# Expert blocks whose token rows travel through DRAM buffers instead of one-hot matmuls, and small loads behind the second weight piece

## The chip, the core and the metric

The kernel runs on one core of one Trainium2 chip. The time is device microseconds (us) of one launch; the number that counts is the median of three runs. Beside the runs there is one execution recorded by the hardware profiler; it has its own time, and all rows below come from it.

The engines are named as in the profile: PE is TensorE (matmuls; PEld its weight loads), DVE is VectorE, ACT is ScalarE, POOL is GpSimd, SP is SyncE, which only issues transfers here. A q behind a name (SPq, POOLq) is that engine's instruction queue.

## The reference

Two decoder layers over 256 tokens of width 1024, all in float32, and a last RMSNorm. Each layer has an attention part (eight stick-breaking heads, four differential heads) and a feed-forward part; the first layer's is a dense SwiGLU of width 2816, the second's a mixture of eight SwiGLU experts of width 3584, of which each token uses two:

```python
logits = xf @ router_w                          # 256 x 8
top_logit, top_idx = lax.top_k(logits, 2)
gates = softmax(top_logit)
# tokens sorted by expert into blocks of 128 rows, each block of one expert
buf = zeros((cap, D)).at[dest].set(xf[sorted_tok])
yb = [swiglu(xb, w_gate[e], w_up[e], w_down[e]) for xb, e in blocks]
y = yb.reshape(cap, D)[dest] * sorted_gate[:, None]
out = segment_sum(y, sorted_tok)                # each token gets its two rows back
```

How many blocks there are depends on the data. With these inputs there are eight: the trace has 112 loads of gate pieces, 14 for each block.

## The kernel before

**Weights.** All weights are read once per use, in pieces of 1 MB (128 partitions x 2048 float32), 401 of them. SP loads them one after the other into a ring of seven buffers (`raw`); piece n is issued when the buffer of piece n-7 has been given back (`load`, line 343). A float32 matmul is done as three fast ones: ACT copies a piece rounded into `w_hi` (`split_hi`, line 327), DVE writes the rest `raw - w_hi` into `w_lo` (`split_lo`, line 332), both into rings of three buffers, and PE runs `mm3` (lines 437 to 439) over hi·hi, lo·hi and hi·lo. The activations are split in the same way (`aT_hi/aT_lo`, `xe_hi/xe_lo`, `he_hi/he_lo`, `ye_hi/ye_lo`).

**Order.** Every engine's program is written out by hand, and the engines meet in semaphores. In the program `piece_used` counts pieces that PE has finished, `lo_ready` those that DVE has split. Piece n can be split when PE has finished piece n-3.

**Start.** SP loads the two tiles of x and then pieces; ACT's queue loads the first gain and all constants (430 KB, with the identity that PE's transposes need); POOL issues ten small loads (bias tables, lambda vectors, head gains).

**Router.** After the last attention of layer 1 DVE normalises the rows (`hn`), PE transposes them (line 477) and forms the logits (line 666), and DVE picks the two experts by some 20 small operations (lines 1246 to 1271). Beside this POOL, ACT and DVE split `hn` into three bfloat16 parts `rows3` (lines 427, 429, 790, 1234), whose sum is exact.

**Expert block.** A block takes 42 pieces in chunks c = 0 to 7: chunk c has the gate and up pieces of 512 hidden columns and the down pieces of the chunk before. Its 128 input rows are gathered by matmuls: `gather` (line 689) multiplies `rows3` with a one-hot matrix `onehot`, 48 bfloat16 matmuls, in chunk 6 of the block before. Its output `ps[4:6]` is split into `ye_hi/ye_lo` and returned by `scatter` (line 698): eight matmuls with the transposed one-hot matrix, four after the second gate piece of the next block (t = 0) and four after its second up piece (t = 1), which need two transposes of `hot32` in chunk 2 (line 748), and two DVE additions into `xs` (`add_back`, line 1330). Block 0 is written out, blocks 1 to 6 are a loop on each engine, block 7 (the last) is written out.

In block 0 DVE works out the gates (chunk 1), the list of blocks (chunk 2) and the columns of each block (chunk 3), between its splits.

Of the kernel before, what the change touches and what calls it, by code (L numbers as in the profile page):

```python
# [19 lines left out]
F32 = mybir.dt.float32  # L20
# [7 lines left out]
P = 128  # L28
# [10 lines left out]
NE = 8  # L39
# [18 lines left out]
MAX_BLOCKS = S * 2 // P + NE - 1  # L58
TAB = MAX_BLOCKS + 1
# [51 lines left out]
def build(nc, x, w_in, w_out, attn_norm, ffn_norm, sb_out_norm, diff_subln, lambda_q1, lambda_k1,  # L111
          lambda_q2, lambda_k2, rel_bias, dense_w_gate, dense_w_up, dense_w_down, router_w,
          expert_w_gate, expert_w_up, expert_w_down, final_norm, consts, out):
    with ExitStack() as ctx:
# [61 lines left out]
        with ExitStack() as phase:  # L176
            hT_hi = sb("hT_hi", [P, FT, S], F32R, phase)
            hT_lo = sb("hT_lo", [P, FT, S], F32R, phase)

        until_experts.close()  # L180
        with ExitStack() as phase:
# [4 lines left out]
            rows3 = se("rows3", [P, 3, TT, D], BF16)  # L186
            onehot = se("onehot", [P, TT, P], BF16)
# [4 lines left out]
            ye_hi = se("ye_hi", [P, D], F32R)  # L192
# [3 lines left out]
            rT = se("rT", [P, KT, S])  # L196
# [28 lines left out]
            gate = se("gate", [P, TT, TAB])  # L225
            ebi = se("ebi", [P, TAB], I32)
            nbi = se("nbi", [P, 1], I32)

        scratch = nc.dram_tensor("bias_scratch", (DF_HEADS, 384), F32, kind="Internal").ap()
        ident = cst[:, C_ID:C_ID + P]  # L230
# [8 lines left out]
        cst_in, small_in, lam_ld, bkt_in = (sem(n) for n in ("cst_in", "small_in", "lam_ld", "bkt_in"))  # L239
        rw_in = sem("rw_in")  # L240
# [22 lines left out]
        part_done, rest_done = sem("part_done"), sem("rest_done")  # L263
# [4 lines left out]
        sc_done, sc_added = [sem("sc_done0"), sem("sc_done1")], [sem("sc_added0"), sem("sc_added1")]  # L268
        hot_t, hot_saved, hot_ready = (sem(n) for n in ("hot_t", "hot_saved", "hot_ready"))
# [69 lines left out]
        def _(sp):  # L339
# [8 lines left out]

            for n, src in enumerate(sources):
# [10 lines left out]
            load_block(0, slice(0, 1))  # L360
            sp.wait_ge(tab_done, 1)
            final = sp.value_load(nbi[0:1, 0:1], min_val=3, max_val=MAX_BLOCKS - 1)
            with sp.Fori(1, final + 1) as b:
                load_block(b, bass.ds(sp.value_load(ebi[0:1, bass.ds(b, 1)], min_val=0, max_val=NE - 1), 1))
            for t in range(TT):
                sp.wait_ge(out_rows, t + 1)
                sp.dma_start(out[0, t * P:t * P + P, :], hn[:, t, :]).then_inc(out_sent, 16)
# [4 lines left out]
        def _(pool):  # L372
            norms = [attn_norm[0], ffn_norm[0], attn_norm[1], ffn_norm[1], final_norm]

            def load_gain(m):
# [3 lines left out]
            pool.dma_start(bkt[:, 0:384], consts[0:N_BUCKETS + 1, C_OH:C_OH + 384]).then_inc(bkt_in, 16)  # L379
            pool.dma_start(bkt[0:N_BUCKETS, 384:384 + DF_HEADS], rel_bias[:, :]).then_inc(bkt_in, 16)  # L380
            pool.dma_start(bkt[N_BUCKETS:N_BUCKETS + 1, 384:384 + DF_HEADS],
                           consts[N_BUCKETS:N_BUCKETS + 1, C_MASKED:C_FLIP]).then_inc(bkt_in, 16)
            pool.dma_start(flip[:], consts[:, C_FLIP:C_END]).then_inc(bkt_in, 16)
            for i, v in enumerate((lambda_q1, lambda_q2, lambda_k1, lambda_k2)):
                pool.dma_start(lam_in[:, i], v.rearrange("l d -> (l d)").partition_broadcast(P)).then_inc(lam_ld, 16)
            pool.dma_start(g_sb[:].rearrange("p l d -> p (l d)"),
                           sb_out_norm.rearrange("l d -> (l d)").partition_broadcast(P)).then_inc(small_in, 16)
            pool.dma_start(g_df[:].rearrange("p l d -> p (l d)"),
                           diff_subln.rearrange("l d -> (l d)").partition_broadcast(P)).then_inc(small_in, 16)
# [14 lines left out]
            for l in range(DEPTH):  # L404
# [14 lines left out]
                if l == 0:  # L419
                    load_gain(2)  # L420
                    load_gain(3)
# [3 lines left out]
            for t in range(TT):  # L425
                pool.wait_ge(rows_done[t], 6)
# [987 lines left out]
```

## Time and profile before

| | us |
|---|---|
| median of the runs | 1552.97 (1551.99 to 1553.61) |
| the profiled execution | 1551.61 |
| its span, first to last instruction | 1549.9 |
| PE busy | 1450.6 (94%) |
| DVE busy | 1163.4 (75%) |
| ACT busy | 937.6 (60%) |
| moved by DMA | 427.52 MB, mean 276 GB/s |

The 1.7 us between span and time lie around the program. The busy shares are means over stages with different limits; the last two thirds of the span, from about 530 us on, are the eight expert blocks. PE's busy time is modelled at the ends of matmuls, so distances between starts say more than durations: a 512-column matmul is given with 0.39 us, and one starts every 0.227 us (883.63, 883.86, 884.09 us and so on). The stretches shown below are, in this order, one block of the loop, 34 us inside it, the start, and the first gather.

### The profile page before, as it was taken

The page shows a single profiled execution, that of the slowest core. Times are in us where ns is not written, and L with a number is a line of the kernel's source. Part 1 is how long each engine was busy: PE and PEld are TensorE (multiplying, and loading weights), DVE is VectorE, ACT ScalarE, POOL GpSimd, SP SyncE. Part 2 cuts the span into 40 slices and gives each one's busy share as a digit, 9 for nine tenths or more (in the row PEclk, how much of TensorE's full clock was granted, in tenths as well). Part 3 has the DMA queues.
Part 4 walks back from the last instruction along what each step waited for, and adds up shares of the span by engine and source line. Part 5 has one row for each costly group of instructions (what it writes and reads, how often), then busy time and mean ns, then how long its engine had stood idle before and what let it go on. Part 6 is the DMA issues. An engine that isn't in the chain of part 4 may idle for free.

```text
span 1549.9 us, 19815 instructions
## 1 busy us (share of the span) xinstructions
PE 1450.6 (94%) x7681; PEld 1226.9 (79%) x7681; DVE 1163.4 (75%) x884; ACT 937.6 (60%) x745; POOL 34.3 (2%) x60
## 2 busy tenths in 40 slices
PE   5997899998989699999999999999999999999996
PEld 4885899988867577778878878878878887887885
DVE  4547555545556799889888888979988988888886
ACT  4344343434444477667677767767766767776774
POOL 1110000000010100000000000000000000000000
PEclk9997999999998899999999999999999999999999
DMA  9641455555421399899989989989999999998991
GB/s 322 207 137 55 150 171 184 189 190 170 157 95 57 128 350 362 316 352 366 358 310 383 365 308 373 373 302 356 378 324 354 368 352 320 375 367 304 375 372 62
DMA packets 183299, 427.52 MB, mean 276 GB/s; under 512 B 6833, under 2 KB 8885, under 8 KB 183248
## 3 DMA queue, kind: packets, MB, share of 16 engines
q1 hardware_dynamic: 181840, 422.60, 76.2%
q0 software_dynamic: 1120, 3.24, 0.7%
q10 hardware_dynamic: 288, 0.96, 0.2%
q8 instruction: 37, 0.61, 0.2%
q14 instruction: 14, 0.11, 0.0%
HBM read 425.72 MB, written 1.05 MB: 275 GB/s over the span
## 4 chain that ended last, share of the span: by engine, by line
PE 87%; DVE 8%; ACT 2%; issue 1%; DMA 1%; ACTq 0%; DVEq 0%; SPq 0%
PE ps L437 27%; PE ps L439 26%; PE ps L438 26%; DVE w_lo L332 3%; PE ps L689 2%; PE ps L718 2%; ACT w_hi L327 1%; DMA raw<-in_w_in 1%; PE ps L698 1%; PE ps L511 1%; PE ps L477 1%; DVE hn L1033 1%; DVE aT_lo L1041 0%; DVE mx L1116 0%; DVE zb L1114 0%
## 5 line engine op out<-in xcount | busy, mean ns | idle before, releaser
L332 DVE TENSOR_TENSOR w_lo<-raw,w_hi 128x2048 fp32r<-128x2048 f32 x401 | 916.0, 2293 | 259.9 <-ACT w_hi L327 259.3
L327 ACT ACTIVATE w_hi<-raw 128x2048 fp32r<-128x2048 f32 x401 | 766.9, 1916 | 374.3 <-PE ps L439 368.3
L437 PE MATMUL ps<-w_hi,xe_hi 128*128 128x512 f32 x896 | 354.2, 395 | 6.8 <-DVE w_lo L332 6.8
L439 PE MATMUL ps<-w_hi,xe_lo 128*128 128x512 f32 x896 | 349.4, 390 | 0.0
L438 PE MATMUL ps<-w_lo,xe_hi 128*128 128x512 f32 x896 | 348.9, 389 | 0.0
L437 PEld LDWEIGHTS ps<-w_hi,xe_hi 128*128 128x128 f32 x896 | 168.3, 188 | 42.9 <-DVE w_lo L332 9.8
L439 PEld LDWEIGHTS ps<-w_hi,xe_lo 128*128 128x128 f32 x896 | 168.2, 188 | 35.7
L438 PEld LDWEIGHTS ps<-w_lo,xe_hi 128*128 128x128 f32 x896 | 168.4, 188 | 33.5
L437 PE MATMUL ps<-w_hi,he_hi 128*128 128x512 f32 x448 | 176.3, 394 | 17.4 <-DVE he_lo L1364 12.0
L437 PE MATMUL ps<-aT_hi,w_hi 128*128 128x256 f32 x608 | 175.0, 288 | 9.3 <-DVE aT_lo L1041 9.3
L439 PE MATMUL ps<-w_hi,he_lo 128*128 128x512 f32 x448 | 174.6, 390 | 0.0
L438 PE MATMUL ps<-w_lo,he_hi 128*128 128x512 f32 x448 | 174.4, 389 | 0.0
L438 PE MATMUL ps<-aT_lo,w_hi 128*128 128x256 f32 x608 | 173.9, 286 | 0.0
L439 PE MATMUL ps<-aT_hi,w_lo 128*128 128x256 f32 x608 | 173.8, 286 | 0.0
L437 PEld LDWEIGHTS ps<-aT_hi,w_hi 128*128 128x128 f32 x608 | 118.7, 195 | 11.5 <-DVE aT_lo L1041 10.4
L438 PEld LDWEIGHTS ps<-aT_lo,w_hi 128*128 128x128 f32 x608 | 118.8, 195 | 0.0
L439 PEld LDWEIGHTS ps<-aT_hi,w_lo 128*128 128x128 f32 x608 | 118.7, 195 | 0.0
L437 PEld LDWEIGHTS ps<-w_hi,he_hi 128*128 128x128 f32 x448 | 84.1, 188 | 40.6 <-issue 13.7
L439 PEld LDWEIGHTS ps<-w_hi,he_lo 128*128 128x128 f32 x448 | 84.1, 188 | 17.8
L438 PEld LDWEIGHTS ps<-w_lo,he_hi 128*128 128x128 f32 x448 | 84.1, 188 | 17.0
L790 ACT ACTIVATE he_hi<-ps 128x512 fp32r<-128x512 f32 x56 | 33.5, 599 | 80.1 <-PE ps L718 80.1
L437 PE MATMUL ps<-w_hi,aT_hi 128*128 128x512 f32 x128 | 50.9, 398 | 3.6 <-DVE aT_lo L1041 3.6
(207 smaller groups left out, 1124.1 us busy)
## 6 DMA issues: line engine op xcount, KB each, us to landing
raw<-in_expert_w_gate SPq DMA_DIRECT2D x112, 1024.0 KB, 6.3
raw<-in_expert_w_up SPq DMA_DIRECT2D x112, 1024.0 KB, 6.6
raw<-in_expert_w_down SPq DMA_DIRECT2D x112, 1024.0 KB, 6.5
raw<-in_w_in SPq DMA_DIRECT2D x24, 1024.0 KB, 6.8
raw<-in_dense_w_gate SPq DMA_DIRECT2D x11, 1024.0 KB, 5.1
raw<-in_dense_w_up SPq DMA_DIRECT2D x11, 1024.0 KB, 5.0
raw<-in_dense_w_down SPq DMA_DIRECT2D x11, 1024.0 KB, 4.9
raw<-in_w_out SPq DMA_DIRECT2D x8, 1024.0 KB, 5.0
```

The lines of the kernel that those rows point to most:

```text
L327: nc.scalar.activation(w_hi[:, n % SPL, :], raw[:, n % RAW, :], ACT.Copy).then_inc(hi_ready, 1)
L332: nc.vector.tensor_tensor(w_lo[:, n % SPL, :], raw[:, n % RAW, :], w_hi[:, n % SPL, :].bitcast(F32), ALU.subtract).then_inc(lo_ready, 1)
L437: pe.matmul(o, s_hi, m_hi, start=start, stop=False, skip_group_check=True)
L438: pe.matmul(o, s_hi, m_lo, start=False, stop=False, skip_group_check=True)
L439: return pe.matmul(o, s_lo, m_hi, start=False, stop=stop, skip_group_check=True)
L477: last = pe.transpose(ps[:, 4 + j, (2 * q + t) * P:(2 * q + t) * P + P], hn[:, t, (2 * j + q) * P:(2 * j + q) * P + P], ident)
L511: pe.matmul(bank[:, 0:ZW], neg_tri, spl[:, g % 2, m, :], start=False, stop=False, skip_group_check=True)
L689: last = pe.matmul(ps[:, 1 + 2 * j, q * P:q * P + P], rows3[:, part, t, k * P:k * P + P], onehot[:, t, :], start=(t == 0 and part == 0), s ...
L698: last = pe.matmul(ps[:, bank + c, :], onehotT[:, t, :], part[:, c * CH:c * CH + CH], start=(part is ye_hi), stop=(part is ye_lo), skip_gr ...
L718: last = pe.transpose(ps[:, 7, f * P:f * P + P], hid[:, c % 2, f * P:f * P + P], ident)
L790: return nc.scalar.activation(dst, src, ACT.Copy, scale=scale)
L1033: V.scalar_tensor_tensor(out=hn[:, t, :], in0=xs[:, t, :], scalar=row_fine[:, t:t + 1], in1=gain[:], op0=ALU.mult, op1=ALU.mult).then_inc( ...
```

## The change

1. `x_rows` and `y_rows` are DRAM buffers of 11 blocks of 128 rows of 4 KB. POOL clears an SBUF tile `zero` in layer 0, and SP fills both buffers with it, two stores of 512 KB behind each of the weight pieces 24 to 34.
2. In block 0 DVE computes for every token the row of its two places (`destinations`, chunk 3) and which of them lie before the last block (`rows_before_last`, chunk 4); the columns of the blocks move from chunk 3 to chunk 5. POOL then sends the rows of `hn` to `x_rows` by four indirect transfers.
3. For blocks 1 to 7 SP loads the block's rows (`xrow`, 512 KB) ahead of piece 32 of the block before, and PE turns them by eight transposes in chunk 6. The 48 matmuls of `gather` go. Block 0 alone is still gathered, by 16 float32 matmuls from `hn` and `hot32`.
4. ACT copies a block's output to `yrow`, and SP stores it to `y_rows` (512 KB) ahead of piece 12 of the next block. The scatter matmuls, `ye_lo`, `hot32`'s transposes, the one-hot tiles and both additions stay for the last block alone. In the last block POOL fetches the tokens' rows of the other blocks by four indirect transfers of 512 KB, and DVE adds them, two in chunk 4 and two in chunk 5.
5. `rows3` and the work on it by POOL, ACT and DVE go.
6. At the start the identity (64 KB) is loaded alone and first on ACT's queue; the other constants (366 KB) stand behind piece 0 on SP's queue, and the ten small loads go from POOL's queue to SP's, behind piece 1.

```diff
+            def small_loads():
+
+                sp.dma_start(bkt[:, 0:384], consts[0:N_BUCKETS + 1, C_OH:C_OH + 384]).then_inc(bkt_in, 16)
...
             for n, src in enumerate(sources):
                 load(n, src)
-
-            def load_block(b, e):
+                if n == 0:
+                    sp.dma_start(cst[:, P:CONSTS], consts[:, P:CONSTS]).then_inc(cst_in, 16)
+                if n == 1:
+                    small_loads()
+                if ZERO_AT <= n < ZERO_AT + MAX_BLOCKS:
+                    sp.wait_ge(zero_set, 1)
+                    sp.dma_start(x_blocks[n - ZERO_AT], zero[:]).then_inc(zeroed, 16)
+                    sp.dma_start(y_blocks[n - ZERO_AT], zero[:]).then_inc(zeroed, 16)
...
+                    if i == Y_STORE and not first:
+
+                        sp.wait_ge(y_saved, b)
+                        sp.dma_start(y_blocks[bass.ds(before, 1)].rearrange("b p d -> (b p) d"), yrow[:]).then_inc(y_sent, 16)
+                    if i == X_LOAD and not last_block:
+
+                        if first:
+                            sp.wait_ge(x_sent, 16 * 2 * TT)
+                        else:
+                            sp.wait_ge(y_sent, b * 16)
+                        sp.wait_ge(ga_done, b * 2 + 2)
+                        sp.dma_start(xrow[:], x_blocks[bass.ds(after, 1)].rearrange("b p d -> (b p) d")).then_inc(xrow_in, 16)
...
-            for t in range(TT):
-                pool.wait_ge(rows_done[t], 6)
-                nc.gpsimd.tensor_copy(rows3[:, 0, t], hn[:, t]).then_inc(part_done, 1)
-            pool.wait_ge(part_done, TT + 1)
-            nc.gpsimd.tensor_tensor(rows3[:, 2], hn[:], rows3[:, 1], ALU.subtract).then_inc(rest_done, 1)
             load_gain(4)
+            pool.wait_ge(zeroed, 32 * MAX_BLOCKS)
+            pool.wait_ge(dest_done, 1)
+            for i in range(2):
+                for t in range(TT):
+                    pool.indirect_dma_start(x_rows, bass.IndirectOffsetOnAxis(ap=dest_i[:, i, t:t + 1], axis=0),
+                                            hn[:, t, :], None).then_inc(x_sent, 16)
...
-            def gather(count):
-
-                pe.wait_ge(hot_ready, count)
+            def turn_gathered(b):
+
+                pe.wait_ge(xrow_in, b * 16 + 16)
+                for j in range(2):
+                    for q in range(4):
+                        k = 4 * j + q
+                        last = pe.transpose(ps[:, 1 + 2 * j, q * P:q * P + P], xrow[:, k * P:k * P + P], ident)
+                    last.then_inc(ga_done, 1)
...
-                    if c == 0 and not first:
-                        pe.wait_ge(y_lo, b)
-                        pe.wait_ge(hot_saved, b)
-                        scatter(0)
-                    if c == 1 and not first:
-                        pe.wait_ge(sc_added[1], b)
...
-                        gather(b + 2)
+                        turn_gathered(b)
...
+            def output_rows(b):
+
+                act.wait_ge(piece_used, nth(MOE0, b))
+                copy(yrow[:], both(ps[:, 4:6, :])).then_inc(y_saved, 1)
...
+            def add_rows(i, t):
+
+                dve.wait_ge(y_got[i][t], 16)
+                link(V.scalar_tensor_tensor(out=xs[:, t, :], in0=y_of[:, i, t, :], scalar=g_in[:, i, t:t + 1],
+                                            in1=xs[:, t, :], op0=ALU.mult, op1=ALU.add))
```

**PE in the loop over blocks, chunk 6**, behind the transposes of the hidden rows (`hid`); `xe_hi`, `xe_lo` are the block's input. First the kernel before:

```order
L718 MATMUL ps<-cst,hid 128x128 x4
L683 REGISTER_ALU
L689 MATMUL ps<-onehot,rows3 128x128 x48
L442 REGISTER_ALU
L437 MATMUL ps<-w_hi,xe_hi 128x512
```

and then the changed one:

```order
L787 MATMUL ps<-cst,hid 128x128 x4
L745 ISA
L749 MATMUL ps<-cst,xrow 128x128 x8
L502 REGISTER_ALU
L497 MATMUL ps<-w_hi,xe_hi 128x512
```

The 48 gather matmuls are replaced by eight transposes of the loaded rows, at the same place.

**DVE at the head of a block in the loop**, chunk 0 and the start of chunk 1; `ye_lo` belongs to the output of the block before, `xs` holds the tokens' sums. First the kernel before:

```order
L332 TENSOR_TENSOR w_lo<-raw,w_hi 128x2048
L1325 TENSOR_TENSOR ye_lo<-ps,ye_hi 128x1024
L331 REGISTER_ALU
L332 TENSOR_TENSOR w_lo<-raw,w_hi 128x2048
L1330 ISA
L1330 SCALAR_TENSOR_TENSOR xs<-ps,gate,xs 128x1024
L331 REGISTER_ALU
L332 TENSOR_TENSOR w_lo<-raw,w_hi 128x2048
```

and then the changed one:

```order
L349 TENSOR_TENSOR w_lo<-raw,w_hi 128x2048
L348 REGISTER_ALU
L349 TENSOR_TENSOR w_lo<-raw,w_hi 128x2048
L348 REGISTER_ALU
L349 TENSOR_TENSOR w_lo<-raw,w_hi 128x2048
```

Nothing stands between the splits any more; the addition for t = 1, which came in chunk 1 before, is gone as well.

**SP at the start**, from the tiles of x to the third weight piece. Before the change the two tiles are followed by the pieces alone. First the kernel before:

```order
L341 DMA xs<-in_x 128x1024 x2
L347 DMA raw<-in_w_in 128x4x512 x12
```

and then the changed one, in full up to piece 2:

```order
L358 DMA xs<-in_x 128x1024 x2
L364 DMA raw<-in_w_in 128x4x512
L383 DMA cst<-in_consts 128x732
L364 DMA raw<-in_w_in 128x4x512
L368 DMA bkt<-in_consts 33x384
L369 DMA bkt<-in_rel_bias 32x4
L370 DMA bkt<-in_consts 1x4
L372 DMA flip<-in_consts 128x128
L374 DMA lam_in<-in_lambda_q1 128x128
L374 DMA lam_in<-in_lambda_q2 128x128
L374 DMA lam_in<-in_lambda_k1 128x128
L374 DMA lam_in<-in_lambda_k2 128x128
L375 DMA g_sb<-in_sb_out_norm 128x128
L377 DMA g_df<-in_diff_subln 128x256
L364 DMA raw<-in_w_in 128x4x512 x10
```

The ten small loads stand ahead of pieces 2 to 11, and the constants ahead of piece 1.

## Rows read from the trace of the kernel before

**Rows 1.** Stretches: us, busy by engine (PE, PEld, DVE, ACT, POOL), PEclk, DMA share, GB/s

```profile
781.00:907.00 126.00, 123.23 (x592) 101.68 (x591) 109.64 (x67) 89.08 (x60) 0.00 (x0) 1.00 0.97 350
816.00:850.00 34.00, 34.00 (x156) 28.21 (x155) 30.24 (x18) 24.97 (x16) 0.00 (x0) 1.00 1.03 385
0.00:17.00 17.00, 3.91 (x16) 3.14 (x16) 3.89 (x11) 4.77 (x10) 5.67 (x14) 1.00 0.87 236
525.00:529.60 4.60, 4.60 (x46) 4.60 (x45) 2.96 (x3) 0.60 (x1) 0.00 (x0) 0.50 0.27 61
```

**Rows 2.** Chain of waits, 880 to 1020 us (start us, us, what)

```profile
886.95 2.68 PE ps L689 x48
...
916.60 2.29 DVE w_lo L332
918.93 0.50 PE ps L437
...
1012.95 2.68 PE ps L689 x48
```

**Rows 3.** PE's timeline (start us, us, ..., in brackets idle before and releaser)

```profile
563.92 0.60 PE L718 MATMUL ps<-cst,hid 128*128 128x128 f32 x4
564.35 0.38 PE L748 MATMUL ps<-cst,hot 128*128 128x128 f32 x2
...
902.55 0.47 PE L437 MATMUL ps<-w_hi,he_hi 128*128 128x512 f32 x1 [1.50 <-DVE he_lo L1364]
...
914.17 0.39 PE L698 MATMUL ps<-ye_hi,onehotT 128*128 128x512 f32 x1
```

**Rows 4.** DVE's timeline, head of a block

```profile
915.39 1.28 DVE L1330 SCALAR_TENSOR_TENSOR xs<-ps,gate,xs 128x1024 f32<-128x1024 f32 x1 [1.31 <-PE ps L698]
```

**Rows 5.** DVE's timeline in the router

```profile
506.82 1.02 DVE L1020 SCALAR_TENSOR_TENSOR row_tmp<-row_rstd 128x1 f32<-128x1 f32 x1
...
517.19 3.92 DVE L1251 TENSOR_TENSOR rk<-eq,cst 128x16 f32<-128x16 f32 x1
...
522.18 0.17 DVE L1251 TENSOR_TENSOR rk<-eq,cst 128x16 f32<-128x16 f32 x1
```

**Rows 6.** POOL's timeline in the router

```profile
517.01 4.07 POOL L429 TENSOR_TENSOR rows<-hn,rows 128x2048 bf16<-128x2048 f32 x1 [6.36 <-ACT rows L790]
521.02 0.56 POOL L377 DMA_DIRECT2D gain<-in_final_norm  x1
```

**Rows 7.** PE's timeline: small float32 matmuls, and the first gather

```profile
476.50 1.06 PE L593 MATMUL ps<-v_df,wT 128*128 128x128 f32 x4
...
524.82 5.23 PE L689 MATMUL ps<-onehot,rows 128*128 128x128 bf16 x48 [1.49 <-DVE onehot L1268]
529.86 0.48 PE L437 MATMUL ps<-w_hi,xe_hi 128*128 128x512 f32 x1
```

**Rows 8.** Timeline of the start

```profile
16.80 1.91 ACT L327 ACTIVATE w_hi<-raw 128x2048 fp32r<-128x2048 f32 x1 [6.04 <-DMA raw<-in_w_in]
...
22.29 0.58 PE L437 MATMUL ps<-aT_hi,w_hi 128*128 128x256 f32 x1 [7.53 <-DVE aT_lo L1041]
```

**Rows 9.** The page: GB/s that the transfers moved, in 40 equal slices of 38.7 us

```profile
GB/s 322 207 137 55 150 171 184 189 190 170 157 95 57 128 350 362 316 352 366 358 310 383 365 308 373 373 302 356 378 324 354 368 352 320 375 367 304 375 372 62
```

**Rows 10.** Block 0, chunk 3: DVE's extra work, and PE behind it

```profile
584.66 0.25 DVE L1311 TENSOR_TENSOR tmpb<-cm,posm 128x96 f32<-128x96 f32 x1
...
587.39 6.70 DVE L332 TENSOR_TENSOR w_lo<-raw,w_hi 128x2048 fp32r<-128x2048 f32 x3
...
589.74 0.50 PE L437 MATMUL ps<-w_hi,he_hi 128*128 128x512 f32 x1 [1.28 <-DVE w_lo L332]
```

**Rows 11.** A piece's way: SP's issue, ACT's use, landing times of one block's pieces

```profile
849.14 0.37 SPq L347 DMA_DIRECT2D raw<-in_expert_w_up  x1
...
864.30 1.92 ACT L327 ACTIVATE w_hi<-raw 128x2048 fp32r<-128x2048 f32 x1 [0.80 <-PE ps L439]
...
DMA to landing us min/median/max: 5.1/7.3/9.1
```

More of the change, by code:

```diff
@@ L58 @@
 MAX_BLOCKS = S * 2 // P + NE - 1
+ZERO_AT = 24
+Y_STORE, X_LOAD = 12, 32
 TAB = MAX_BLOCKS + 1
@@ L185, in build @@
             xe_lo = se("xe_lo", [P, KT, P], F32R)
-            rows3 = se("rows3", [P, 3, TT, D], BF16)
-            onehot = se("onehot", [P, TT, P], BF16)
+            y_of = se("y_of", [P, 2, TT, D])
+            ye_hi = se("ye_hi", [P, D], F32R)
+            with ExitStack() as router:
+                rT = sb("rT", [P, KT, S], F32, router)
+            xrow = se("xrow", [P, D])
+            yrow = se("yrow", [P, D])
             hot32 = se("hot32", [P, TT, P])
@@ L420, in _ @@
                     load_gain(2)
+                    nc.gpsimd.memset(zero[:], 0.0).then_inc(zero_set, 1)
                     load_gain(3)
@@ L687, in gather @@
                         for t in range(TT):
-                            for part in range(3):
-                                last = pe.matmul(ps[:, 1 + 2 * j, q * P:q * P + P], rows3[:, part, t, k * P:k * P + P],
-                                                 onehot[:, t, :], start=(t == 0 and part == 0), stop=(t == 1 and part == 2),
-                                                 skip_group_check=True)
+                            last = pe.matmul(ps[:, 1 + 2 * j, q * P:q * P + P], hn[:, t, k * P:k * P + P],
+                                             hot32[:, t, :], start=(t == 0), stop=(t == TT - 1), skip_group_check=True)
                     last.then_inc(ga_done, 1)
@@ L754, in expert_block @@
                         expert_in("up", c, 1)
-                    if c == 0 and not first:
-                        pe.wait_ge(sc_added[0], b)
-                        scatter(1)
+                    if c == 1 and not first:
+                        pe.wait_ge(y_saved, b)
                     if c > 0:
@@ L1354, in expert_block @@
                         lo_of("up", c, 0)
-                        if c == 0 and not first:
-                            add_back(b, 0).then_inc(sc_added[0], 1)
                         lo_of("up", c, 1)
@@ L1373, in expert_block @@
                     if first and c == 3:
+                        destinations()
+                    if first and c == 4:
+                        rows_before_last()
+                    if first and c == 5:
                         block_columns()
-                    if c == 4 and not last_block:
-                        one_hot(lambda t: sel[:, t, bass.ds(b + 1, 1)])
+                    if last_block and c in (4, 5):
+                        for t in range(TT):
+                            add_rows(c - 4, t)
                     if 0 < c < E_CH:
```

133 lines of the change are left out of this document (84 added, 49 removed).

## The prediction

> **What bounds the kernel now.** I began with the stretches. One block of the loop lasts 126 us with PE busy for 123.2, DVE for 109.6, ACT for 89.1, and the DMA engines at a share of 0.97 with 350 GB/s [rows 1]. So PE sets the pace, DVE has some 13% to spare, and the transfers have little: that is the first thing to see here. Then the chain of waits: it lies on PE in the blocks, and the gathers of two neighbouring blocks start at 886.95 and 1012.95, 126.00 us apart [rows 2]. Whatever leaves PE's program in a block therefore shortens the kernel seven times, as long as the splits (ACT, then DVE) and the transfers keep up. Last, PE's timeline shows where it stands idle in a block: 1.50 us at the end, for `he_lo` [rows 3], and about 1.1 us at the head, for a split [rows 2].
>
> **Head of a block (7 times).** At 914.17 PE starts the four matmuls of the first scatter [rows 3], and only at 918.93 the second up piece [rows 2]. Between them lies one piece, 12 matmuls at 0.227 = 2.72 us. So 4.76 - 2.72 = 2.04 us go: 0.91 for the scatter and 1.13 of waiting for the split that DVE starts at 916.60 [rows 2], behind the addition at 915.39 [rows 4]. The second scatter is another 4 x 0.227 = 0.91 us. Does the wait come back in another form? DVE had been idle for 1.31 us before 915.39, so the split of the first up piece was done at 914.1; PE now comes for it at 914.17. The next split would end at 914.1 + 2.3 = 916.4, and PE needs it at 914.17 + 2.72 = 916.9. It just fits. ACT's copy of the output stays (into `yrow` instead of `ye_hi`, the same size). Gain 2.95 us, x7 = 20.7. The end with the wait left in place is 1.82 x 7 = 12.7.
>
> **Chunk 6 (7 times).** 48 matmuls take 2.68 us [rows 2]. Eight transposes of 128x128 float32 take 0.108 us each, since four of them on `hid` run from 563.92 to 564.35 [rows 3]: 0.86 us. Gain 1.82, x7 = 12.7. The two transposes of the one-hot tile in chunk 2, of the same kind [rows 3], go too: 0.22 x 7 = 1.5. At half speed the eight would take 1.7 us, which would leave 6.8 of the 12.7.
>
> The 1.50 us at a block's end stay: transposes, `he_hi`, `he_lo` are not touched.
>
> **Router (once).** POOL's subtraction runs from 517.01 to 521.08 [rows 6], and DVE's `rk`, 128x16, lasts 3.92 us beside it where its twin lasts 0.17 [rows 5]. `row_tmp`, of one column, lasts 1.02 us [rows 5] beside POOL's first cast; I give it the same 0.17 without. Both stand on the way from the norm to the logits and the choice. With POOL's work gone I take off 3.75 + 0.85 = 4.6 us. POOL's issue of a transfer does not do this: 521.02 to 521.58 [rows 6] DVE's small steps keep their length. Against it stands the first gather. Before, 48 bfloat16 matmuls from 524.82 to 529.86 [rows 7], at the 1.2 GHz level (PEclk 0.50, [rows 1]); at the 2.4 GHz level they take 2.68 [rows 2]. PE had had little to do before. The new one has 16 float32 matmuls of 128x128, each of two records (line 593 is such a product, and its two matmuls are x4 in [rows 7]). A record of this size takes 0.108 at the high level [rows 3] and so 0.216 at the low one: 32 of them 6.9 us, 1.8 more than before, or 3.5, 1.6 less. PE idles for some 4 us less now, so either is possible; I take the low level. Net -2.8 (the other end -6.2).
>
> **Start (once).** PE's first weight matmul starts at 22.29, 5.5 us behind ACT's first split, which had waited for piece 0 until 16.80 [rows 8]. Ahead of or beside this piece everything flowed: x, a gain, the constants, ten small loads. Now 1 MB of x, 512 KB of gain, the identity's 64 KB and the piece stand there, 2.69 MB. At the 322 GB/s of the first slice [rows 9], and with data from about 2 us on, the piece lands at 10.4; I take 10.5, so 6.3 earlier. Ends: at the 385 GB/s of the blocks 9.0 (-7.8); at the 236 that the first 17 us had, small packets among them [rows 1], 13.4 (-3.4). x's second tile comes earlier by its share, and the row norms finish just ahead of the split. The small loads stand behind pieces 0 and 1 and land by about 18 us; PE first asks for the bias tables behind the two pieces of its first product, DVE for the lambda vectors behind three splits: in time. Piece 2 follows at about 20 us and is needed when PE has done two pieces, 96 matmuls, behind 16 us: in time too.
>
> **What is added.** The 22 stores of zeros, 11.5 MB behind 11 pieces, double the load of a stage that moves 184 to 190 GB/s [rows 9]. 380 at most is just below the 385 of [rows 1], and seven buffers at 5.5 us a piece are far ahead there: nothing (to 2). Clearing `zero` on POOL may hold DVE up once, as the cast did: 0.2 (0 to 1). In block 0 the extra steps of chunk 3 took 587.39 - 584.66 = 2.73 us and made PE wait 1.28 [rows 10], so 1.45 us in a chunk cost nothing. `destinations` has 7 steps of 0.2 (0.17 and the hand-over), `rows_before_last` 4: both fit, and the block columns cost in chunk 5 what they cost in chunk 3: 0 (to 1.5). In the last block DVE adds two rows of 1.28 us [rows 4] in each of two chunks: 2.56 - 1.45 = 1.1, x2 = +2.2 (0 to 5).
>
> The waits that are new stand on SP and POOL. Behind SP's wait for `x_sent` all weight pieces from 32 on are queued. POOL can send from about 586 us, SP arrives some 16 us later, six pieces on; four transfers of 512 KB at an issue of 0.56 each [rows 6] and 9.1 us to land [rows 11] need 11 to 12, or 17 if they share the engines evenly with the weights. If they are late by a few us, the ring covers it: a piece issued at 849.14 is taken by ACT at 864.30, 15.2 us later, and takes 7.3 to land, 9.1 at worst [rows 11]. In the last block POOL's fetch has over 25 us before DVE asks for it.
>
> **Sum.** -20.7 - 12.7 - 1.5 - 2.8 - 6.3 + 0.2 + 0 + 2.2 = -41.6. The profiled execution, 1551.61 us, would be 1510.0; the median of the runs is 1.36 above it, and I predict 1552.97 - 41.6 = **1511.4**.
>
> **Rivals.** *The transfers become the bound.* A block now moves 42 pieces and two half pieces, 45.1 MB, and is to last 126.0 - 5.0 = 121.0 us: 373 GB/s. For it speaks the row of the block: 350 GB/s at a share of 0.97 is 361 at full share, which gives 124.9 us a block, only 1.1 gained. Against it: 385 GB/s for 34 us on end, at a share of 1.03, so the share is no ceiling [rows 1]; and the slack of 6 to 8 us of [rows 11]. At 385 the block needs 117 us of transfers. With 361 the three block terms shrink from 34.9 to 7.7 and the time is 1538. The Trainium skill says in DMA: Bandwidth & Descriptors, section "Where 436 GB/s comes from", that HBM gives a core about 358 GB/s and that this binds; by it a block would take 126.0 us and nothing would be gained in the blocks, 1546. By that rule the 385 of this trace could not be; its section on measured bandwidth allows more with the other core idle, as here, and the trace agrees with that.
>
> *A split takes the place of the wait at the head.* The fit is 0.1 and 0.5 us. If DVE is late there as before, 1.13 x 7 = 7.9 comes back: 1519.
>
> *Slower than before.* POOL issues the indirect transfers, each to 128 addresses that it must take one by one from a table. What that costs is shown by no row. If the four take T us from 586 on, SP holds all weights back and PE starves once T is over 16 + 8 = 24 us. It outweighs the 41.6 from T = 66 on, 16 us for each transfer, where the nearest row has 0.56 for an issue of 128 rows. At T = 80 the time would be 1511.4 + 56 = 1567.
>
> *The change does not do what it says*, say PE waits for `xrow` in each block: SP issues that load ten pieces ahead, 29 us, so I give it nothing of its own.
>
> **How the numbers follow.** Forecast 0.66 (its own range 1505 to 1520), split late 0.12 (1519), transfers bound 0.14 (1520 to 1546, mostly 1538), slower 0.04, faster than forecast (gather at the high level, start at 385 GB/s) 0.04, about 1505. The range 1504 to 1528 leaves out nearly all of the slow case, most of the transfer case and a little below. About 0.2% is what a measurement tells from no change. Faster 0.95, same 0.01, slower 0.04.
>
> **What would show it.** ACT's first split near 10.5 us and PE's first weight matmul near 16. `rk` at 0.17 us. Blocks of the loop 121 us apart, with no wait at the head and 1.50 us at the end. The wait of ACT's splits for `raw` in the blocks: none, if I am right; some in each block, growing to the last, if the transfers bind. Idle of about 1.1 us on PE twice in the last block. Wrong would be a distance of blocks of 125 or more, or SP waiting long at `x_sent`.

## The result and the profile after

The changed kernel takes 1511.17 us (median of 4 runs, 1510.65 to 1512.92) against 1553.29 (4 runs, 1551.99 to 1554.19): a ratio of 0.973, 95% interval 0.9715 to 0.9748. Predicted were 1511.4 with a range of 1504 to 1528. The profiled execution took 1511.28 with a span of 1509.5, against 1551.61 and 1549.9; the steps below are taken from these two.

The same place of PE's program, in both traces (us from the span's start; the lead is the difference):

| PE's start of | before | after | lead |
|---|---|---|---|
| first weight matmul | 22.29 | 15.91 | 6.38 |
| last weight matmul ahead of the router | 503.64 | 498.85 | 4.79 |
| transposes of the logits | 516.25 | 510.62 | 5.63 |
| first gather | 524.82 | 515.35 | 9.47 |
| first weight matmul of block 0 | 529.86 | 521.55 | 8.31 |
| last hidden tile of block 0 | 648.45 | 638.19 | 10.26 |
| first hidden tile of block 1 | 676.16 | 662.91 | 13.25 |
| first hidden tile of the last block | 1432.08 | 1388.64 | 43.44 |
| last hidden tile of the last block | 1527.66 | 1487.34 | 40.32 |

So nearly all of it comes from the blocks. From one block of the loop to the next it is 120.95 us, as against 126.00 in [rows 2] (121.0 was predicted). Stretches of the trace after: one block, 34 us inside one, and the start (engines' busy time and, last, PEclk, DMA share and GB/s), to be read against [rows 1]:

```profile
882.22:1003.19 120.97, 119.13 (x541) 98.10 (x541) 105.14 (x58) 89.05 (x60) 0.00 (x0) 1.00 1.01 373
789.00:823.00 34.00, 34.00 (x156) 28.14 (x155) 30.10 (x18) 25.16 (x17) 0.00 (x0) 1.00 1.04 395
0.00:17.00 17.00, 4.53 (x21) 4.02 (x22) 8.48 (x17) 10.29 (x15) 0.20 (x4) 0.96 0.81 268
```

PE is busy for 119.1 of 121.0 us, and the transfers run at the 373 GB/s that the new pace needs. The waits from 640 to 1390 us, which are the end of block 0 and the six blocks of the loop (what waited and for whom; total, times, longest):

```profile
ACT w_hi L344 <- PE ps L499: 115.9, 184, 1.2
...
PE ps L497 <- DVE he_lo L1436: 10.5, 7, 1.5
...
PE ps L497 <- DVE w_lo L349: 2.2, 7, 0.3
```

No split waits for `raw`. What is left on PE is the stop of 1.5 us at each block's end, which [rows 3] showed and which was not touched, and a short one behind it. The start, on the chain of waits (start, us, what), answers to [rows 8]:

```profile
1.72 8.63 DMA raw<-in_w_in
10.38 1.92 ACT w_hi L344
12.32 2.29 DVE w_lo L349
14.61 1.21 DVE aT_lo L1105 x2
15.91 0.55 PE ps L497
```

The router on DVE, to be read against [rows 5]; `row_tmp` and `rk` now last what their twins did:

```profile
502.02 0.16 DVE L1084 SCALAR_TENSOR_TENSOR row_tmp<-row_rstd 128x1 f32<-128x1 f32 x1
...
511.57 0.17 DVE L1312 TENSOR_TENSOR rk<-eq,cst 128x16 f32<-128x16 f32 x1
```

POOL's timeline at the indirect transfers, the operation that no row of before showed, and SP's wait for them:

```profile
578.41 2.20 POOL L476 DMA_INDIRECT x_rows<-hn,dest_i  x1 [73.67 <-DVE dest_i L1370]
580.92 1.86 POOL L476 DMA_INDIRECT x_rows<-hn,dest_i  x1 [0.30 <-issue]
583.08 1.99 POOL L476 DMA_INDIRECT x_rows<-hn,dest_i  x1 [0.30 <-issue]
585.38 2.58 POOL L476 DMA_INDIRECT x_rows<-hn,dest_i  x1 [0.30 <-issue]
```

```profile
SPq L407 <- DMA x_rows<-hn,dest_i: 3.4, 1, 3.4
```

An issue costs 1.9 to 2.6 us, three to five times the 0.56 of [rows 6]. From the first issue to the last landing, 596.1, it is 17.7 us. The ring hides it, but barely: the weight piece issued at 597.0, right behind SP's wait, landed at 610.4 and ACT took it at 611.0, 0.6 us later. In the loop this slack is 5.1 to 13.6 us. Most of it was gone before SP waited: the pieces issued at 581.9 to 589.9, while the rows were on their way, had 1.0 to 1.1 us left when they landed. From 588 to 597 us the transfers moved 412 GB/s.

Last, the end of the chain in the last block, where rows are added (start, us, what):

```profile
1440.92 0.68 DVE he_lo L1436
1441.60 1.20 DVE xs L1382
1442.83 1.30 DVE xs L1382
1444.24 2.30 DVE w_lo L349
1446.58 0.50 PE ps L497
```

The chunk with this stop lasts 18.32 us where its neighbours last 16.81, and the next one 18.37: 3.1 us in all, which is the step down from 43.44 to 40.32 in the table.

### The profile page after: what moved, and what is told of

Read it like the earlier page. It is cut to its first block, busy times and chain, and to the rows that moved or that the text cites. A ratio compares the mean times of both kernels' runs of the same rounds, so it can differ in the third digit from the quotient of the medians.

```text
span 1509.5 us, 19091 instructions
## 1 busy us (share of the span) xinstructions
PE 1421.4 (94%) x7315; PEld 1199.9 (79%) x7315; DVE 1130.3 (75%) x842; ACT 935.7 (62%) x744; POOL 42.6 (3%) x58
## 4 chain that ended last, share of the span: by engine, by line
PE 87%; DVE 8%; ACT 2%; issue 1%; DMA 1%; ACTq 0%; SPq 0%; DVEq 0%
PE ps L497 28%; PE ps L499 27%; PE ps L498 27%; DVE w_lo L349 3%; ACT w_hi L344 2%; PE ps L787 1%; PE ps L573 1%; DVE aT_lo L1105 1%; DMA raw<-in_w_in 1%; DVE hn L1097 1%; PE ps L537 0%; PE ps L759 0%; DVE mx L1180 0%; DVE zb L1178 0%; PE ps L749 0%
## 5 line engine op out<-in xcount | busy, mean ns | idle before, releaser
L497 PE MATMUL ps<-w_hi,he_hi 128*128 128x512 f32 x448 | 176.8, 395 | 19.8 <-DVE he_lo L1436 12.0
```

Of the source, the lines that this page charges most:

```text
L497: pe.matmul(o, s_hi, m_hi, start=start, stop=False, skip_group_check=True)
```

## The experiments

Each was run 5 times if nothing else is said, beside the kernel before on the same chip. The medians of that are 1553.56 for start_only, pool_router, head_add and spread, 1554.12 for extra2, extra4, early and early_spread, and 1552.95, on another chip, for start_cst, send_thrice, more_zeros and busy_router. The changed kernel was not run again in these groups; what is said against it is against its 1511.17 above. As the kernel before moved by 1.2 us from group to group, a difference of about 1 us between medians of different groups says nothing by itself.

| run | us | lowest to highest | ratio to before, 95% |
|---|---|---|---|
| start_only | 1548.07 | 1545.5 to 1548.61 | 0.9942 to 0.9970 |
| start_cst (11 runs) | 1552.26 | 1549.27 to 1554.71 | 0.9987 to 1.0005 |
| pool_router | 1515.86 | 1514.59 to 1516.97 | 0.9743 to 0.9770 |
| head_add | 1514.83 | 1514.58 to 1515.74 | 0.9738 to 0.9765 |
| spread | 1508.74 | 1507.65 to 1509.55 | 0.9695 to 0.9722 |
| extra2 | 1510.57 | 1507.88 to 1512.47 | 0.9709 to 0.9735 |
| extra4 (4 runs) | 1534.01 | 1532.44 to 1535.66 | 0.9858 to 0.9888 |
| send_thrice | 1521.76 | 1520.62 to 1523.22 | 0.9782 to 0.9808 |
| more_zeros | 1512.33 | 1510.87 to 1513.27 | 0.9721 to 0.9747 |
| early | 1491.85 | 1488.61 to 1494.37 | 0.9584 to 0.9613 |
| early_spread | 1489.14 | 1486.36 to 1490.76 | 0.9568 to 0.9594 |
| busy_router | 1487.44 | 1486.80 to 1487.53 | 0.9562 to 0.9588 |

**The start alone (start_only).** The kernel before, with

```
                 load(n, src)
+                if n == 0:
+                    sp.dma_start(cst[:, P:CONSTS], consts[:, P:CONSTS]).then_inc(cst_in, 16)
+                if n == 1:
+                    small_loads()
...
+            act.dma_start(cst[:, C_ID:C_ID + P], consts[:, C_ID:C_ID + P]).then_inc(ident_in, 16)
             act.dma_start(gain[:], attn_norm[0].partition_broadcast(P)).then_inc(gain_first, 16)
-            act.dma_start(cst[:], consts[:, 0:CONSTS]).then_inc(cst_in, 16)
```

and without the ten small loads on POOL's queue.

> The kernel before with the start of the changed one and nothing else. Theory: the first piece and the small loads stood in each other's way; PE's first weight matmul moves from 22.29 to about 15.9 (6.4 us). Of that the changed kernel still has 5.65 at its router, and I put the 0.7 that it loses on the way to the clock's windows, which fall otherwise over the attention; then this kernel loses them too and ends 5.6 us below the kernel before, near 1547.7. Rival: the 0.7 was taken by the zeros (clearing the tile, 22 stores), which are not here; then it ends 6.4 to 7 below, near 1546.5. Second rival: the start's gain needs the changed kernel's other tiles; then no first split near 10.4 here.

PE's first weight matmul came at 15.97 and the median is 5.5 us below before, near the 5.6 expected; on the way the trace lost more than the 0.7 that this rested on. The zeros are not in it, and yet of the 6.3 us of lead only 3.9 stood at the last weight matmul ahead of the router (499.71 against 503.64). So the rival with the zeros falls; the lead is lost elsewhere, see the clock below.

**Which part of the start (start_cst).** As above, without `small_loads()` in SP's queue: the ten small loads stay with POOL.

> The kernel before, with the identity loaded by itself and the other constants behind piece 0, but the ten small loads still on POOL's queue at the start. It tells apart what of the 6.3 us is due to the constants (366 KB moved back) and what to the small loads. Theory of the prediction (all bytes that flow beside the piece count alike, at 322 GB/s): 366 KB are 1.2 us, so ACT's first split comes at about 15.6 in place of 16.80, and the small loads, 0.58 MB, take the rest, most of it because they are small. Rival: the constants held the piece back by more than their bytes, and the split comes at 12 to 13.

ACT's timeline of this run:

```profile
16.14 1.91 ACT L328 ACTIVATE w_hi<-raw 128x2048 fp32r<-128x2048 f32 x1 [6.75 <-DMA raw<-in_w_in]
```

0.66 us earlier than 16.80 [rows 8]; start_only has this step at 10.44. So 5.7 of the 6.4 us come from where the small loads stood. At 322 GB/s their 0.58 MB would be 1.8 us: they cost three times that. Whether that is because they were issued beside the piece or because POOL's queue carried them is not told apart, since start_only changes both. In the medians start_cst can't be told from before. My expectation, which counted bytes, had the split at 15.6. The prediction itself did not hang on this: it took the 16.80 of before as it stood and gave the new start, in which no small load is left ahead of the piece, the rate of the first slice. The piece landed at 10.35 and 10.4 was worked out.

**POOL beside DVE (pool_router).** The changed kernel with POOL's old work in the router, into a tile that nobody reads:

```
+            for t in range(TT):
+                pool.wait_ge(rows_done[t], 6)
+                nc.gpsimd.tensor_copy(cast[:, 0, t], hn[:, t]).then_inc(cast_done, 1)
+            pool.wait_ge(lg_done, 1)
+            pool.wait_ge(cast_done, 2)
+            nc.gpsimd.tensor_tensor(cast[:, 1], hn[:], cast[:, 0], ALU.subtract).then_inc(cast_done, 1)
```

> The changed kernel, with POOL's two casts and its subtraction of 128x2048 put back in the router (into a tile that nobody reads). Theory: a step of DVE that meets POOL's subtraction is held until it ends; one DVE step of the choice lasts about 3.9 us again and one step of the norm about 1.0, so +4.6 us, near 1515.8. The clock may take or give about 1.5 of it at the first gather. Rival: rk was long for another reason (its place in the chain, the wait for the logits), and POOL costs nothing: 1511.2.

+4.7 us, as expected. DVE's and POOL's timelines of this run:

```profile
510.62 0.17 DVE L1319 TENSOR_REDUCE m<-lg 128x2 f32<-128x16 f32 x1
510.83 3.72 DVE L1320 TENSOR_TENSOR eq<-lg,m 128x16 f32<-128x16 f32 x1
514.58 0.17 DVE L1321 TENSOR_TENSOR rk<-eq,cst 128x16 f32<-128x16 f32 x1
```

```profile
510.46 4.05 POOL L478 TENSOR_TENSOR y_of<-hn,y_of 128x2048 bf16<-128x2048 f32 x1 [6.01 <-PE ps L741]
```

This time `eq` is held and `rk` is not, so it is no property of `rk`: the tensor-tensor step that meets POOL's subtraction ends with it (514.55 and 514.51; spans on POOL are rough). The reduction at 510.62 runs within POOL's instruction at its usual 0.17. The Trainium skill, SBUF — State Buffer, section "Terms", says that the port pair which DVE and GpSimd share is held for a whole instruction and that the loser fully blocks; the rows of `eq` and of POOL's subtraction agree.

**The wait at the head (head_add).** In the blocks of the loop, behind the split of the first up piece:

```
+                        if c == 0 and not first and not last_block:
+                            V.scalar_tensor_tensor(out=y_of[:, 0, 0, :], in0=xs[:, 0, :], scalar=gate[:, 0, 0:1],
+                                                   in1=xs[:, 1, :], op0=ALU.mult, op1=ALU.add)
```

> The changed kernel, with one step of DVE of 1.28 us (an addition of 128x1024 that nobody reads) behind the split of the first up piece in each of the six blocks of the loop, where the addition of the scatter stood, and no scatter. Theory: DVE has 0.1 us to spare at the first up piece and 0.5 at the second, so PE waits 1.28 - 0.5 = 0.8 for the second: 6 x 0.8 = +4.8 us, near 1516.0. Rival: the wait of 1.13 at the head came from the hand-over between PE's scatter and DVE, not from DVE's time; then nothing here, 1511.2. Second rival: DVE never makes the step up before the block ends; then 1.28 x 6 = 7.7, near 1518.9.

Blocks of the loop are 121.63 to 121.67 us apart against 120.95 to 120.97: 0.70 each, +3.7 us in the medians. PE's timeline of this run:

```profile
1019.34 0.50 PE L497 MATMUL ps<-w_hi,xe_hi 128*128 128x512 f32 x1 [0.38 <-DVE w_lo L349]
```

The expectation had 0.8 each. So the wait was DVE's time, and DVE has 0.6 us to spare there (0.5 was read). The rest of the old 1.13, 0.4 us, I put to DVE's having to wait for PE's scatter, 1.31 us in [rows 4]; no run shows that part by itself.

**Additions and columns spread (spread).**

```
-                    if first and c == 5:
-                        block_columns()
-                    if last_block and c in (4, 5):
-                        for t in range(TT):
-                            add_rows(c - 4, t)
+                    if first and c in (5, 6):
+                        block_columns(c - 5)
+                    if last_block and c in (3, 4, 5, 6):
+                        add_rows((c - 3) // TT, (c - 3) % TT)
```

> The changed kernel, with one row added in each of the chunks 3 to 6 of the last block instead of two in chunks 4 and 5, and the block columns of block 0 half in chunk 5 and half in chunk 6. Theory: a chunk hides 1.45 us of DVE's time, and one addition takes 1.28 and half of the columns 1.37; then the two stops of about 1.55 each in the last block and the one in block 0 all go: -4.6 us, near 1506.6. Rival: DVE has no such spare time in a chunk, its debt passes on to the next piece; then the four stops are of about 0.8 each and the time stays near 1511.

Measured: -2.4 us in the medians, and in the trace -3.6 behind the start of block 0. The chunks of the last block last 16.99 to 17.05 in place of 18.35, with 16.81 undisturbed, and chunk 5 of block 0 17.04 in place of 18.38. So a chunk hides about 1.1 us of DVE's time, not 1.45. That figure had been 2.73 - 1.28 from [rows 10]; but the chunk there was 1.58 longer than its neighbours. A row's bracket counts idle time from the modelled end of the matmul before, 0.39 behind its start, where the next one would have started after 0.23; and the pair of matmuls behind a stop is 0.34 apart, not 0.23. Both are left out of the 1.28. 2.73 - 1.58 is 1.15, and 2.64 - 1.15 is the 1.5 us of each stop in the last block.

**How much the transfers carry (extra2, extra4).** Two and four more loads of 1 MB in each of the blocks 0 to 6:

```
+                    if i in places and not last_block:
+                        j = places.index(i)
+                        ...
+                        sp.dma_start(y_of[:, j % 2], edown_v[0, :, 0:2, :]).then_inc(extra_in, 16)
```

> The changed kernel, with two more transfers of 1 MB in each of the blocks 0 to 6 (weights that nobody reads, into the buffer of the rows that come back, which lies idle there). A block then moves 47.2 MB in 120.95 us, 390 GB/s, against 373. Theory (transfers were never the bound, and can sustain about the 385 to 397 GB/s of the best slices): the ring of seven pieces loses its slack, PE waits at most 1 us a block: 1511 to 1518. Rival (361 GB/s is the ceiling, and the changed kernel lives on slack from before): 47.2 / 361 = 130.8 us a block, +69 us, near 1580.

> As before with four more transfers of 1 MB in each of the blocks 0 to 6: 49.3 MB, 408 GB/s if the block stayed at 120.95 us. Theory: this is above what any slice showed (397); at 397 a block takes 124.2 us, +3.2 x 7 = +23, near 1534. If the engines could carry well over 400, nothing happens: 1511. At 385 it is 128.1 us a block, +50, 1561. The time gives the ceiling itself.

The stretch from 640 to 1360 us, first of extra2, then of extra4:

```profile
640.00:1360.00 720.00, 710.86 (x3223) 585.91 (x3224) 626.73 (x345) 529.92 (x351) 0.00 (x0) 1.00 1.03 392
```

```profile
640.00:1360.00 720.00, 698.20 (x3126) 565.59 (x3127) 607.68 (x335) 518.23 (x342) 0.00 (x0) 1.00 1.04 396
```

With two more, blocks stay 120.95 us apart at 392 GB/s. With four they take 124.1 to 124.35, and the splits wait for `raw`, as this row of extra4's waits has it:

```profile
ACT w_hi L346 <- DMA raw<-in_expert_w_up: 58.5, 40, 3.4
```

49.3 MB in 124.1 to 124.35 us are 396 to 397 GB/s, and that is what these loads of 1 MB sustain. That 1534 came out to the microsecond is luck in part: the forecast had seven blocks of +3.2, while the trace has six of +3.2 to +3.4, 1.0 in the last block and 1.1 ahead of block 0. The changed kernel at 373 stands 6% below the limit. The rival at 361 is refuted. The Trainium skill, Perfetto Trace Analysis, section "Roofline", takes about 120% of 358 GB/s as the practical ceiling of a core alone. That is 430 GB/s, an estimate from its figures; here the limit in pieces of 1 MB was 397, 111%, though for 20 us of send_thrice, below, the transfers moved 415.

**The indirect transfers (send_thrice).**

```
-                            sp.wait_ge(x_sent, 16 * 2 * TT)
+                            sp.wait_ge(x_sent, 16 * 6 * TT)
...
-            for i in range(2):
-                for t in range(TT):
-                    pool.indirect_dma_start(x_rows, ...)
+            for rows in (x_rows2, x_rows3, x_rows):
+                for i in range(2):
+                    for t in range(TT):
+                        pool.indirect_dma_start(rows, ...)
```

> The changed kernel, with the four indirect transfers of token rows issued three times (twice into other DRAM buffers that nobody reads, then into x_rows); SP waits for all twelve. In the changed kernel an issue takes 1.9 to 2.6 us and the last of four lands about 10 us after it, SP waits 3.4 us, and the pieces behind it land 0.6 us before ACT takes them, against 7 in other chunks: the cover was nearly used up. Theory of the prediction (SP is held until the last transfer has landed, and the ring gives that time back only up to the piece's landing): twelve issues end at 608, the last lands at about 617, and the piece that SP then issues is wanted by ACT at 608.7 and takes 8 to land: PE stands 16 us, 1527. Rival (only the bytes count: 4.2 MB more at 397 GB/s): +10.6, 1522. Second rival: the ring has more to give than I read, under +5, 1515.

+10.6 us, where the theory said 16; block 0 to block 1 is 134.17 us in place of 124.89, +9.3. SP's wait (19.8 us in place of 3.4):

```profile
SPq L409 <- DMA x_rows<-hn,dest_i: 19.8, 1, 19.8
```

SP came free at 613.7 rather than 617, and its first piece landed at 619.6, 5.9 us later and not 8. Block 0 starts 1.8 us later in this execution, so ACT would have taken the piece at 610.5: 9.1 us late, close to the 9.3 measured. But SP's wait made little of that. ACT already stood for three pieces that SP had issued at 586.0, 588.9 and 591.6, ahead of its wait:

```profile
603.40 1.92 ACT L346 ACTIVATE w_hi<-raw 128x2048 fp32r<-128x2048 f32 x1 [2.33 <-DMA raw<-in_expert_w_gate]
609.82 1.92 ACT L346 ACTIVATE w_hi<-raw 128x2048 fp32r<-128x2048 f32 x1 [4.50 <-DMA raw<-in_expert_w_up]
614.53 1.91 ACT L346 ACTIVATE w_hi<-raw 128x2048 fp32r<-128x2048 f32 x1 [2.79 <-DMA raw<-in_expert_w_up]
```

By the same reckoning the third of them was 7.6 us late. Meanwhile the transfers ran without a pause, and only then did SP's wait leave them short of work (590 to 610 us, and 610 to 614):

```profile
590.00:610.00 20.00, 19.03 (x86) 15.42 (x85) 14.73 (x12) 10.74 (x8) 14.15 (x8) 1.00 1.04 415
610.00:614.00 4.00, 1.20 (x8) 0.78 (x6) 2.23 (x1) 1.74 (x1) 0.00 (x0) 1.00 0.60 241
```

So the rows' bytes, ahead of or among the weights', made about 7.6 of the 9.3 us, as the rival had it, and the theory's hold of SP at most the 1.7 left. An estimate from these rows fits: the 4.2 MB added are 10.1 us at 415 GB/s, less the 1.0 of slack. POOL's eight further issues do not set the time here, since the transfers were never idle behind them. Two stretches at the low clock, from 614.9 and from 625.1, each behind a stop of PE, are part of what was lost. Shown is that the slack of the changed kernel at this place was used up.

**More zeros (more_zeros).** A third store beside each round of two, into a buffer that nobody reads:

```
+                    sp.dma_start(spare_blocks[n - ZERO_AT], zero[:]).then_inc(zeroed, 16)
```

> The changed kernel, with 11 more stores of zeros (17.3 MB in 33 stores in place of 11.5 in 22, the third of each round into a buffer that nobody reads). Theory: 11 pieces and 33 stores are 28.8 MB, 73 us at 397 GB/s, on 60 us of PE's work; the ring is 12 us behind after it, and it had some 38 to spare in this stage, so nothing changes: 1511. Rival: the stage is near its limit already and the 22 stores cost the changed kernel something; then the 11 more cost up to 12 us.

1512.33: no difference that can be told. From the first weight matmuls of the stage at 170 us to the ones at 368 it is 198.4 us in both traces. The stores are free, with room.

**The stop that was left (early, early_spread).** In chunk 6 PE now runs

```
                     if c > 0:
                         expert_down(c - 1, 0)
+                        if c == E_CH - 1:
+                            turn_hidden(c)
                         expert_down(c - 1, 1)
```

with `he_hi` and `he_lo` of this one tile in the idle halves of `ye_lo`, and each half of `gathered` moved behind `he_lo` and behind the last split.

> The changed kernel, with the last hidden tile of a block transposed between the two pieces of the down product before it (in buffers of its own), so that he_hi and he_lo are made while PE works; ACT's and DVE's halves of the next gathered tile are moved behind it. Theory: the two stops that stayed at the end of a block, 1.55 us for he_lo and 0.47 for the next split, are hand-over and not DVE's load, so they go: 2.0 x 8 = -16 us, near 1495. A block then lasts 118.9 us and needs 379 GB/s, which the transfers carry. Rival: DVE has no time to spare there (six splits of 2.29, hid, he_lo and two gathered halves on 16.3 us of PE's work), and what goes at he_lo comes back at the next two or three splits: half of it, near 1503. If a block's transfers bind at 373 GB/s: nothing, 1511.

> The run before together with the spread additions and block columns. Theory: the two do not touch the same chunks but one (chunk 6), so the gains add: 2.4 for the spread as measured and up to 16: near 1493. Rival: the last addition and half of the columns now stand in the chunk in which the early transposes use up DVE's spare time, and about 1 us of it comes back.

1491.85, 19.3 us below the changed kernel; 1489.14 with the spreading. Blocks are 118.6 us apart: 2.35 us less each rather than 2.0. Some 0.15 of the rest lies in the pair of matmuls behind a stop, whose distance is 0.31 to 0.34 where it is 0.23 elsewhere; the last 0.2 I can't place. PE's timeline of early, where 1.50 us of idle time stood:

```profile
990.36 0.40 PE L505 MATMUL ps<-w_hi,he_lo 128*128 128x512 f32 x1
990.59 0.60 PE L793 MATMUL ps<-cst,hid 128*128 128x128 f32 x4
990.95 0.47 PE L503 MATMUL ps<-w_hi,he_hi 128*128 128x512 f32 x1
```

and 640 to 1360 us of early, in which PE has no idle time at all:

```profile
640.00:1360.00 720.00, 720.00 (x3278) 595.32 (x3277) 636.88 (x353) 541.29 (x359) 0.00 (x0) 1.00 1.03 381
```

**The clock in the router (busy_router).** early_spread with products that nobody reads in PE's pauses, such as

```
+                if l == DEPTH - 1:
+                    for _ in range(12):
+                        pe.matmul(ps[:, 7, :], aT_hi[:, 0, 0:P], aT_hi[:, 0:2, :].rearrange("p a s -> p (a s)"),
+                                  start=True, stop=True, skip_group_check=True)
                 turn_rows(3 * l + 2)
```

> The kernel of the run early_spread, with 24 products that nobody reads where PE waits in the router: 12 ahead of the last transposes, 8 behind the transposes of the logits, 4 ahead of the first gather. In early_spread the granted clock falls to 0.5 from 504.0 to 507.4 and from 514.2 to 521.1, and the first gather takes 6.2 us there. Theory: PE did little before each fall, and with these products the clock stays at 1.0; the gather takes 3.5 and the logits' product about 1 less: -3.7 us, near 1485.5. Rival: the added products stand ahead of the real ones and delay them by more than the clock gives, or the clock falls all the same: 1489 to 1491.

From the last weight matmul ahead of the router to the first of block 0, first busy_router, then early_spread:

```profile
499.84:519.48 19.64, 18.11 (x109) 13.81 (x108) 13.53 (x36) 8.36 (x16) 1.50 (x2) 1.00 0.42 137
```

```profile
499.09:521.76 22.67, 14.39 (x73) 10.51 (x72) 13.53 (x36) 8.34 (x16) 1.50 (x2) 0.77 0.48 158
```

```profile
515.99 3.73 PE L773 MATMUL ps<-hot,hn 128*128 128x128 f32 x32
```

The clock stays at the high level, the gather takes 3.5 us from start to start in place of 6.2, and the stretch is 3.0 us shorter; 1.0 more was lost because the last four products stood ahead of the gather (router 5.7 us in place of 4.7). In the medians it is -1.7, where -3.7 was expected. Against their own runs of before the two ratios overlap (0.9562 to 0.9588 and 0.9568 to 0.9594), so the medians alone don't show a gain; the trace does, at this stretch. The five runs lie within 0.7 us where the five of early_spread, on another chip, lie within 4.4. It is the lowest median of all: 1487.44.

## Why the prediction was right

| term | predicted | measured in the traces |
|---|---|---|
| start, with the clearing of `zero` | -6.1 | -6.4 at PE's first product, -4.8 at the router |
| router | -2.8 | -3.5 |
| heads of blocks, 7 | -20.7 | -20.9 |
| chunk 6 of a block, 7 | -12.7 | -13.0 |
| one-hot transposes | -1.5 | -1.2 in blocks 1 to 6 |
| steps in block 0 | 0 | -0.1, with its own one-hot transposes |
| last block | +2.2 | +3.1 |
| sum | -41.6 | -40.4, with the start at the router |

That 1511.4 lies 0.2 us from the median is luck: the router gave 0.7 more than forecast, the start 1.3 less, the last block cost 0.9 more, and two executions of one kernel differ by more than that. What was right is the list of terms and the size of the large ones.

*Blocks.* The mechanism and the size hold: matmuls that leave PE's program leave the time, since neither the transfers (extra2) nor DVE (head_add) are in the way. The fit at the head, 0.1 and 0.5 us, was real: 0.6 is measured at the second piece.

*Router.* `rk` gave 3.84, `row_tmp` 0.86, the gather cost 1.16 in place of 1.8, since the clock rose before it ended. That the gather runs at the low level was right:

```profile
514.03:520.86 6.83, 5.51 (x26) 5.51 (x27) 4.02 (x8) 1.78 (x2) 0.00 (x0) 0.50 0.35 103
```

*Start.* The size at PE was right, its reason only in part (start_cst). What failed is the silent step that a lead at the start is kept to the end: 1.6 of 6.4 us were gone at the router. Ahead of the router nothing but the start and the zeros differs, and the zeros are free. The lead first grew to 7.8, most of it by 30 us: in before the 256-column matmuls start 0.21 us apart until 28.0, in after only until 19.0, and 0.12 afterwards (this stretch of before is not low in its PEclk). Then it fell to 6.2 and, in the second layer, from 6.4 to 4.9. What differs is where the low level of the clock falls, here on weight matmuls of the output projection of either layer, which in before ran at the high level (before has PEclk 1.00 from 137.33 and from 478.66):

```profile
131.74:135.15 3.41, 3.41 (x9) 2.64 (x8) 2.73 (x9) 0.51 (x2) 0.00 (x0) 0.50 0.74 276
473.07:476.49 3.42, 3.42 (x10) 2.64 (x9) 2.73 (x9) 0.51 (x2) 0.00 (x0) 0.50 0.79 285
```

PE was busy for 4.0 of the 6.8 us just before the first and 3.9 before the second. Nine of the kernels run here have the same instructions up to the router but for the zeros, and their first weight matmul comes between 15.9 and 16.1 us; yet block 0 starts between 518.0 and 523.4. Followed along their weight matmuls, their leads over each other change, but for 0.3 us in all, only across stretches of the low clock, which lie at other places in each. So 5 us of chance lie in a profiled execution of this kernel. The gain by medians, 42.1, and by the two profiled executions, 40.3, differ by less.

*Last block.* Mis-sized: 3.1, not 2.2, because the cover of a chunk is 1.15 us, not 1.45 (spread).

*Transfers.* No cost, as predicted, but the margin at the indirect ones was 0.6 us, not the several that I had in mind. An issue took 2.2 us, not 0.56; the 17 us for transfers that share evenly with the weights came out at 17.7. The prediction looked for the danger in SP's hold. The traces show it in the pieces already issued, which landed later while the rows moved (send_thrice). Of the rivals none came about.

## What to carry to other kernels

Where one engine's program sets the pace, count what leaves it, instruction by instruction, and then look for the engine that has the least to spare at that very place. Take the price of a stop from the distance between starts, not from the idle time in a row's bracket. A few small loads beside the first big one can cost several times their bytes. Where a ring of loads must hide other transfers, look at the landing of the pieces already issued, not only at the queue that waits. And a short pause of PE is paid for again in the matmuls behind it.

## What the runs showed of the hardware that was not expected

- The loads of one core, in pieces of 1 MB, sustain 396 GB/s over 720 us (extra4); 392 cost nothing (extra2). Beside indirect stores it was 415 for 20 us (send_thrice).
- Indirect stores of 128 rows of 4 KB: 1.9 to 2.6 us for an issue on POOL (1.0 to 2.6 with twelve in a row); with eight more of them the kernel took 10.6 us longer.
- A DVE tensor-tensor step on 16 columns lasts as long as POOL's subtraction beside it (3.72 and 3.92 us in place of 0.17), while a DVE reduction inside the same POOL instruction lasted 0.17.
- Ten small loads, 0.58 MB, on POOL's queue beside a 1 MB piece held it back by 5.7 us, against the same loads behind the second piece on SP's.
- The same program differs by up to 5.4 us at the same place through where the granted clock is low. Products in PE's pauses held it high in the router; the five runs lay within 0.7 us in place of 4.4, which five runs on two chips do not settle.
